# Hybrid decoder step: ten ring slots, convolution tables between weight parts, query rows behind loads, another order in the last attention step, Strassen blocks loaded in the projection

## Chip, cores and metric

The kernel runs on one core of one Trainium2 chip. The metric is the device time of one launch in microseconds (us).

## The reference

One layer (D_MODEL 1024, float32) for a prompt of 512 tokens and for 64 sample tokens (8 sequences of 8 tokens with a past of 4096 keys in pages). Cut to what matters:

```python
x = x + 0.5 * swiglu_ffn(rms_norm(x, g_ffn1), w_ffn1_in, w_ffn1_out)      # D_FF 2816
h = rms_norm(x, g_mix)
u, q, k, v, qi, ki, wi, gc, ga = project_in(h, w_in, g_q, g_k, pos)
conv = silu(layer_norm(depthwise31(u, state), g_cln, b_cln)) @ w_cout
idx  = top_k(index_scores(qi, wi, keys), k=min(256, n_keys // 4))        # a search by threshold
att  = gathered_attention(q, K[idx], V[idx]) @ w_aout                    # 8 heads x 64
x = x + (gc * conv + ga * att) @ w_o
x = x + 0.5 * swiglu_ffn(rms_norm(x, g_ffn2), w_ffn2_in, w_ffn2_out)
```

The new keys, values, indexer keys and the last rows of the convolution's input are outputs too.

## The kernel before

Every engine has one instruction stream written out by hand (the blocks `sp`, `pe`, `act`, `dve`, `pool`); nothing is scheduled by a planner. Semaphores order the engines, and what stands ahead of a waiting instruction on its engine decides when it runs. In order of time:

**A, 0 to 160 us, sample tokens.** The 64 sample tokens go through the first feed-forward part and `w_in`. The weights are read once, as 82 loads of 512 KB (`w_in`'s first four are smaller), which SyncE issues in `stream` (L369) into a ring of 6 slots; each waits until TensorE has used the load six places ahead of it (`ring_used`). TensorE multiplies them in `stream_mm` (L577). Between them it also transposes the prompt (`xnp`), sums its squares (L565) and transposes the cached indexer keys (`turn_ik`, L713). `x_sample` and the prompt's four blocks of 512 KB are issued at the start, by ScalarE.

**B, 160 to 208 us.** The sample tokens' index scores on TensorE.

**C, 205 to 652 us, prompt feed-forward 1**, as 68 units of 1024 weight columns by 128 rows, in three thirds. Each float32 weight is split in two parts of fewer bits, so a unit is a chain: SyncE's `load` (L377) brings `w_raw`, ScalarE (`hi`, L1234) makes `w_hi`, GpSimd (`lo`, L2547) or, in the last third, VectorE (`split_lo`, L1722) makes `w_lo`, and TensorE (L589) does three sets of products. `w_raw` has two slots, `w_lo` two. VectorE meanwhile runs the top-k search, and then, from unit 47 on, the keys of the sample attention: per token a product `kprod` (L2257) of gathered keys `kv` (GpSimd, L2613) with query rows `qb` (SyncE, L442), and a sum. The list `KEYS` gives the unit at which each token's turn comes, and `queries` in SyncE's stream sends the next row when the unit is far enough; four `qb` buffers, so a row waits on `kv_used`. UA = 68 is the first number after these units.

**D, 652 to 1106 us.** The projection of the prompt by `w_in` (`wn`, L969, L1003, L1116), attention of the prompt in 32 steps (logits, softmax on ScalarE as `Pp`, its transposes `pTp` from L1140, values L1150), and the convolution's taps on VectorE.

**E, 1106 to 1228 us.** Eight merge units (L544) for `w_aout` and `w_cout`, the convolution's layer norm (sums over channels by TensorE, L1159; `conv_mean_off` on VectorE, L2443 and L2445), and eight units of `w_o`. `t_hi` and `t_lo` are the parts of the attention's output `attT`.

**F, 1228 to 1634 us.** Feed-forward 2 with Strassen's seven products (L638) for ten blocks; GpSimd makes sums of weight blocks in `left_sums` (L2657 to L2667), VectorE splits them (L1749, L1754).

## Time and profile before

| | |
|---|---|
| median of 3 runs (lowest, highest) | 1648.18 us (1648.09, 1651.65) |
| the profiled execution | 1649.05 us, span of its records 1647.1 us |
| mean granted TensorE clock | 0.962 |
| PE busy / DVE / POOL / ACT | 1505.0 (91%) / 1105.2 (67%) / 574.4 (35%) / 497.9 us (30%) |
| DMA | 248.77 MB, 151 GB/s over the span |

PE is TensorE (matmuls), PEld its weight loads, DVE VectorE, ACT ScalarE, POOL GpSimd, SPq SyncE's DMA queue. A row `[9.06 <-POOL w_lo L2547]` says that the engine was idle 9.06 us before this instruction, and that w_lo, made by line 2547 on POOL, ended that. The difference of 1.95 us between the profiled execution's time and its span lies outside the records.

### The profile page before, as it was taken

The numbers are of one execution on the slowest core, as the hardware profiler recorded it, in microseconds if no ns is written. First come the engines' busy times: TensorE is split into PE (matmuls) and PEld (weight loads), VectorE is DVE, ScalarE is ACT, GpSimd is POOL, SyncE is SP. The second block draws the span as 40 slices with busy tenths as digits, with TensorE's granted clock in tenths as the row PEclk, the third lists the DMA queues.
The fourth block names the chain that finished last, engine by engine and source line by source line (L and its number), as shares of the span: only waits on it lengthen the run. The fifth ranks groups of instructions, "written<-read, shape, count | busy, mean of one in ns | idle before, by whom it ended". The sixth has DMA issues, their size and how long they took to land.

```text
span 1647.1 us, 20847 instructions
## 1 busy us (share of the span) xinstructions
PE 1505.0 (91%) x8219; PEld 1161.4 (71%) x8219; DVE 1105.2 (67%) x1688; ACT 497.9 (30%) x748; POOL 574.4 (35%) x412
## 2 busy tenths in 40 slices
PE   5877979889999987999999889978998899999998
PEld 2332358767888865544766555658998899999997
DVE  1615269999994688899868689843769755565222
ACT  3411422112211213122121444453346444454110
POOL 2000244335435855646216477112122355430000
PEclk9988989999999998999999899989999999999999
DMA  9897143222224787878528677232231222322222
GB/s 314 314 346 247 39 52 102 90 67 87 91 77 138 252 255 240 290 246 300 184 77 271 215 236 210 84 122 72 90 116 63 82 88 89 102 78 70 75 94 77
DMA packets 156275, 248.77 MB, mean 151 GB/s; under 512 B 11885, under 2 KB 104253, under 8 KB 155915
## 3 DMA queue, kind: packets, MB, share of 16 engines
q1 hardware_dynamic: 131006, 163.96, 31.0%
q0 software_dynamic: 23104, 76.16, 14.7%
q10 hardware_dynamic: 2069, 7.34, 1.2%
q8 instruction: 64, 1.05, 0.3%
q14 instruction: 32, 0.26, 0.0%
HBM read 237.58 MB, written 10.20 MB: 150 GB/s over the span
## 4 chain that ended last, share of the span: by engine, by line
PE 65%; DVE 17%; DMA 8%; issue 3%; ACT 3%; POOL 2%; ACTq 0%; SPq 0%; DVEq 0%; POOLq 0%
PE ps L638 13%; PE ps L589 11%; PE ps L654 8%; PE ps L1003 6%; PE ps L544 6%; PE ps L969 5%; DVE EQ L2103 4%; PE ps L1116 3%; DVE yacc L2419 2%; PE ps L783 2%; PE ps L577 2%; DVE kprod L2257 2%; DMA ring<-w_ffn_in 2%; PE ps L1020 1%; DMA w_raw<-w_ffn_out 1%
## 5 line engine op out<-in xcount | busy, mean ns | idle before, releaser
L2547 POOL TENSOR_TENSOR w_lo<-w_raw,w_hi 128x1024 fp32r<-128x1024 f32 x65 | 165.9, 2554 | 302.0 <-ACT w_hi L1234 301.8
L638 PE MATMUL ps<-bh,wqr 128*128 128x288 f32 x944 | 207.7, 297 | 4.5 <-DVE bl L1754 4.5
L1234 ACT ACTIVATE w_hi<-w_raw 128x1024 fp32r<-128x1024 f32 x88 | 91.4, 1040 | 351.5 <-PE ps L589 240.3
L2613 POOL DMA_INDIRECT kv<-cache_k,idxT x128 | 137.8, 1076 | 94.9 <-DVE kprod L2257 62.7
L2613 POOL DMA_INDIRECT kv<-cache_v,idxT x128 | 129.1, 1009 | 102.0 <-PE ps L1020 66.3
L638 PEld LDWEIGHTS ps<-bh,wqr 128*128 128x128 f32 x944 | 158.4, 190 | 4.7 <-issue 4.7
L589 PE MATMUL ps<-h_hi,w_hi 128*128 128x512 f32 x352 | 140.5, 399 | 12.7 <-POOL w_lo L2547 10.0
L589 PE MATMUL ps<-h_hi,w_lo 128*128 128x512 f32 x352 | 138.5, 394 | 0.0
L589 PE MATMUL ps<-h_lo,w_hi 128*128 128x512 f32 x352 | 138.4, 393 | 0.0
L654 PE MATMUL ps<-a_hi,wqr 128*128 128x288 f32 x704 | 121.6, 295 | 0.0
L1003 PE MATMUL ps<-h,wn 128*128 128x288 f32 x448 | 112.6, 412 | 3.1 <-DVE U_p L2089 1.9
L638 PE MATMUL ps<-bl,wqr 128*128 128x288 f32 x384 | 113.8, 296 | 0.0
L969 PE MATMUL ps<-wn,xg 128*128 128x512 f32 (+1 forms) x256 | 105.1, 570 | 3.6 <-DMA wn<-w_in 1.8
L1003 PEld LDWEIGHTS ps<-h,wn 128*128 128x128 f32 x448 | 85.5, 192 | 30.2 <-ACT sgb L1510 2.6
L654 PEld LDWEIGHTS ps<-a_hi,wqr 128*128 128x128 f32 x704 | 103.0, 188 | 0.0
L589 PE MATMUL ps<-a1h,w_hi 128*128 128x512 f32 x176 | 74.7, 424 | 22.9 <-DVE w_lo L1722 10.5
L969 PEld LDWEIGHTS ps<-wn,xg 128*128 128x128 f32 x256 | 49.7, 197 | 56.7 <-issue 49.6
L1762 DVE TENSOR_TENSOR wqr<-wq,wqr 128x1024 fp32r<-128x1024 f32 (+1 forms) x24 | 27.2, 1134 | 91.9 <-ACT wqr L1272 91.9
L589 PEld LDWEIGHTS ps<-h_hi,w_hi 128*128 128x128 f32 x352 | 67.1, 191 | 29.1 <-POOL w_lo L2547 10.6
L2657 POOL TENSOR_TENSOR wq<-wq 128x1024 f32<-128x1024 f32 x10 | 25.5, 2554 | 177.8 <-PE ps L638 135.2
L2257 DVE TENSOR_TENSOR kprod<-kv,qb 128x1024 f32<-128x1024 f32 x64 | 79.8, 1246 | 8.8 <-issue 2.7
L1116 PE MATMUL ps<-h,wn 128*128 128x288 f32 x320 | 84.4, 418 | 0.7 <-ACT sgb L1596 0.7
(477 smaller groups left out, 3288.8 us busy)
## 6 DMA issues: line engine op xcount, KB each, us to landing
w_raw<-w_ffn_in SPq DMA_DIRECT2D x48, 512.0 KB, 3.5
ring<-w_ffn_in SPq DMA_DIRECT2D x44, 512.0 KB, 7.0
wq<-w_ffn_in SPq DMA_DIRECT2D x40, 512.0 KB, 3.6
...
```

The costliest lines, as they stand in the source:

```text
L544: mm = pe.matmul(ps[:, 4 * half + 2 * m + hf_, 0:HALF], w[:, k, m * P:(m + 1) * P], x[:, kc0 + k, hf_ * HALF:(hf_ + 1) * HALF], start=(fir ...
L589: mm = pe.matmul(ps[:, 2 * half + m, :], w[:, k, m * P:(m + 1) * P], x[:, kc0 + k, c0:c0 + SEQ], start=(first and k == 0 and fst), stop=(l ...
L638: mm = pe.matmul(ps[:, bank + m, 0:HALF], w[:, k, m * P:(m + 1) * P], b[:, j, k, :], start=(j in (0, 1, 5) and k == 0 and fst), stop=(k == ...
L654: mm = pe.matmul(ps[:, 4 * half + 2 * m + hf_, 0:HALF], w[:, k, m * P:(m + 1) * P], x[:, kc0 + k, hf_ * HALF:(hf_ + 1) * HALF], start=(kc0 ...
L969: mm = pe.matmul(ps[:, s % 8, 0:n], xg[:, kk, P * b:P * b + P], wt[:, k, :], start=(kk == 0), stop=(kk == KD - 1))
L1003: mm = pe.matmul(ps[:, 4 * half + 2 * m + hf_, 0:HALF], wt[:, k, m * P:(m + 1) * P], h32[:, 4 * (n % 2) + k, hf_ * HALF:(hf_ + 1) * HALF], ...
L1116: mm = pe.matmul(ps[:, 2 * m + hf_, 0:HALF], wt[:, k, m * P:(m + 1) * P], h32[:, 4 * (n % 2) + k, hf_ * HALF:(hf_ + 1) * HALF], start=(n % ...
L1234: act.activation(w_hi[:, slot, 0:n], w_raw[:, slot, 0:n], ACT.Copy).then_inc(S_("hi_ready"), 1)
L2103: return dve.tensor_scalar(EQ[:, :], S[:, :], thr, 0.0, op, ALU.add, accum_out=dst)
L2257: dve.tensor_tensor(kprod[:, :, :], kv[:, n % KV, :, :], qb[:, j, :].unsqueeze(1).to_broadcast([P, 2, DA]), ALU.mult)\
L2547: pool.tensor_tensor(w_lo[:, slot, 0:n], w_raw[:, slot, 0:n], w_hi[:, slot, 0:n].bitcast(F32), ALU.subtract)\
L2613: pool.indirect_dma_start(kv[:, n % KV, c, :], None, rows[n // NS], bass.IndirectOffsetOnAxis(ap=idxT[:, c, t:t + 1], axis=0))\
```

## The change

**1. Stream of stage A.** The first 60 loads go around ten places instead of six: the ring's six, two in `w_raw`, and two in a new `spare` that lies over `w_lo`. The last 22 use the ring's six. `x_sample` is issued by SyncE ahead of the loads; the prompt's four blocks are issued by ScalarE after it has normed the sample tokens.

**2. Tables on GpSimd.** The four loads of the convolution's weights `wconv` (128 x 31 elements of 4 bytes), three small ones and a copy in HBM stand between the `lo` parts of units 4 to 9, not ahead of the one of unit 2.

**3. Query rows.** The row of `KEYS[n]` is sent from unit `KEYS[n]+4` on instead of `+3` (as long as that is below UA). VectorE's `prod(10)` comes ahead of the split of unit 61 (`w_lo`), not behind it.

**4. Last attention step.** On PE the convolution's sums come one step later; on ACT the last gate's high half and the `w_hi` of merge unit 1 come later, and that of merge unit 3 ahead of the four pairs of `silu` and `c_hi`; on DVE `t_lo` comes ahead of `conv_mean_off`.

**5. Strassen blocks.** The first four blocks (`wq`) are loaded behind six of the eight `w_o` loads, not behind all; their wait (`m_ready` 9) is the same.

**6.** `left_sums(2)` on GpSimd waits also for the seventh `bl` of block 1 (`h_ready`).

**7.** Some semaphores are merged with others (`qrep_ready`, `ends_taken`, `unat_done`, `state_kept`).

```diff
+        (spare,), _ = place(used["w_lo"][0], [("spare", (P, 2, 1024), F32)])
+        WIDE = 60
+        RING_AT = [i % 10 for i in range(WIDE)] + [i % RING for i in range(N_RING - WIDE)]
+        def ring_slot(i):
+            s = RING_AT[i]
+            return ring[:, s, :] if s < RING else (w_raw, spare)[(s - RING) // 2][:, (s - RING) % 2, :]
...
-                if i >= RING:
-                    sp.wait_ge(S_("ring_used"), i - RING + 1)
+                if RING_AT[i] in RING_AT[:i]:
+                    sp.wait_ge(S_("ring_used"), i - RING_AT[:i][::-1].index(RING_AT[i]))
...
-                while sent[0] < NS and (u >= ROWS_AT + 5 if sent[0] < 4 else KEYS[sent[0] - 4] + 3 <= u):
+                while sent[0] < NS and (u >= ROWS_AT + 5 if sent[0] < 4 else KEYS[sent[0] - 4] + (4 if KEYS[sent[0] - 4] + 4 < UA else 3) <= u):
...
+                if i == 2:
+                    sp.wait_ge(S_("m_ready"), KD + 1)
+                    for slot, kh, nh in ((A11, 0, 0), (A21[1], 0, 1), (A22[1], 1, 1), (A12[1], 1, 0)):
+                        sp.dma_start(wq[:, slot, :]...).then_inc(S_("w11_in"), 16)
...
-                if i == 33:
+                if i == 34:
                     pe.wait_ge(S_("mix_free"), 10)
                     conv_sums(0, yacc)
...
-            for b in range(4):
-                act.dma_start(xnp[:, b, :], inp["x_prompt"][P * b:P * (b + 1)]).then_inc(S_("xp_in"), 16)
...
             sample_norm(0)
+            for b in range(4):
+                act.dma_start(xnp[:, b, :], inp["x_prompt"][P * b:P * (b + 1)]).then_inc(S_("xp_in"), 16)
...
+                if i == 33:
+                    gate_high(7)
...
+            act.wait_ge(S_("ring_used"), N_RING + 39)
+            hi(UM + 1)
...
+                if v == out_unit(2, 0) - 1:
+                    prod(10)
...
-            conv_mean_off()
             for k in range(KA):
                 dve.wait_ge(S_("parts_hi"), k + 1)
                 dve.tensor_tensor(t_lo[:, k, :], attT[:, k, :], t_hi[:, k, :].bitcast(F32), ALU.subtract).then_inc(S_("t_ready"), 1)
+            conv_mean_off()
...
+                if 4 <= u < 4 + KC:
+                    pool.dma_start(wconv[:, u - 4, :], ...)
...
+                if i == 2:
+                    pool.wait_ge(S_("h_ready"), 2 * KD + 7)
```

GpSimd's stream at the start of stage C, before (`w_lo` is the part that `lo` makes, the first being that of unit 2; line numbers are each kernel's own):

```order
L2593 DMA causal<-c_causal 128x128
L2595 DMA wconv<-w_dw 128x31x1 x4
L2598 DMA bconv<-b_dw 128x4x1
L2598 DMA gcln<-g_cln 128x4x1
L2598 DMA bcln<-b_cln 128x4x1
L2599 DMA o_conv_sample<-state_conv 8x11264
L2547 TENSOR_TENSOR w_lo<-w_raw,w_hi 128x1024 [waits hi_ready] x46
```

And after:

```order
L2566 TENSOR_TENSOR w_lo<-w_raw,w_hi 128x1024 [waits hi_ready] x3
L2633 DMA wconv<-w_dw 128x31x1
L2566 TENSOR_TENSOR w_lo<-w_raw,w_hi 128x1024 [waits hi_ready]
L2633 DMA wconv<-w_dw 128x31x1
L2566 TENSOR_TENSOR w_lo<-w_raw,w_hi 128x1024 [waits hi_ready]
L2633 DMA wconv<-w_dw 128x31x1
L2566 TENSOR_TENSOR w_lo<-w_raw,w_hi 128x1024 [waits hi_ready]
L2633 DMA wconv<-w_dw 128x31x1
L2566 TENSOR_TENSOR w_lo<-w_raw,w_hi 128x1024 [waits hi_ready]
L2637 DMA bconv<-b_dw 128x4x1
L2637 DMA gcln<-g_cln 128x4x1
L2637 DMA bcln<-b_cln 128x4x1
```

Three parts now stand ahead of the first table, and one between each two of the next.

SyncE's stream in the last third of stage C, before (`w_ffn_out` with 4 x 256 and 2 x 256 columns are the two units of an output group, `qb` a query row):

```order
L442 DMA qb<-q_scratch 128x512 [waits kv_used]
L377 DMA w_raw<-w_ffn_out 128x4x256 [waits lo_ready]
L442 DMA qb<-q_scratch 128x512 [waits kv_used] x2
L377 DMA w_raw<-w_ffn_out 128x2x256 [waits lo_ready]
L442 DMA qb<-q_scratch 128x512 [waits kv_used] x2
L377 DMA w_raw<-w_ffn_out 128x4x256 [waits lo_ready]
L442 DMA qb<-q_scratch 128x512 [waits kv_used]
L377 DMA w_raw<-w_ffn_out 128x2x256 [waits lo_ready]
```

And after:

```order
L457 DMA qb<-q_scratch 128x512 [waits kv_used]
L394 DMA w_raw<-w_ffn_out 128x4x256 [waits lo_ready]
L457 DMA qb<-q_scratch 128x512 [waits kv_used]
L394 DMA w_raw<-w_ffn_out 128x2x256 [waits lo_ready]
L457 DMA qb<-q_scratch 128x512 [waits kv_used] x2
L394 DMA w_raw<-w_ffn_out 128x4x256 [waits lo_ready]
L457 DMA qb<-q_scratch 128x512 [waits kv_used] x2
L394 DMA w_raw<-w_ffn_out 128x2x256 [waits lo_ready]
```

Each row stands one load further back.

ScalarE's stream at the last attention step, before (`Pp` and `pTp` of the last two steps, `sgb` and `gate_scratch` the gate's high half, `attT` the attention's output):

```order
L1618 ACTIVATE pTp<-ps 128x512 [waits patt_done,pturn_done]
L1596 ACT_TABLE_LOAD
L1596 ACTIVATE sgb<-ps 128x576 [waits ring_used]
L1548 DMA gate_scratch<-sgb 128x1152 [waits mix_free,sgb_ready]
L1234 ACTIVATE w_hi<-w_raw 128x1024 [waits unit_used,raw1,ring_used]
L1611 ACTIVATE Pp<-Pp,small 128x512 [waits psum_ready]
L1618 ACTIVATE pTp<-ps 128x512 [waits patt_done,pturn_done]
L1624 ACTIVATE attT<-ps 128x128 [waits patt_done]
L1618 ACTIVATE pTp<-ps 128x512 [waits patt_done,pturn_done]
L1624 ACTIVATE attT<-ps 128x128 [waits patt_done]
L1654 ACTIVATE t_hi<-attT 128x576 [waits patt_evac,atts_evac]
L1654 ACTIVATE t_hi<-attT 128x576 x3
```

And after:

```order
L1635 ACTIVATE pTp<-ps 128x512 [waits patt_done,pturn_done]
L1628 ACTIVATE Pp<-Pp,small 128x512 [waits psum_ready]
L1635 ACTIVATE pTp<-ps 128x512 [waits patt_done,pturn_done]
L1641 ACTIVATE attT<-ps 128x128 [waits patt_done]
L1635 ACTIVATE pTp<-ps 128x512 [waits patt_done,pturn_done]
L1613 ACT_TABLE_LOAD
L1613 ACTIVATE sgb<-ps 128x576 [waits ring_used]
L1565 DMA gate_scratch<-sgb 128x1152 [waits mix_free,sgb_ready]
L1641 ACTIVATE attT<-ps 128x128 [waits patt_done]
L1669 ACTIVATE t_hi<-attT 128x576 [waits patt_evac,atts_evac]
L1669 ACTIVATE t_hi<-attT 128x576 x3
L1252 ACTIVATE w_hi<-w_raw 128x1024 [waits unit_used,raw1,ring_used]
```

The gate's table load, `sgb` and `w_hi` stood ahead of the last `Pp`; now the gate stands behind the last `pTp`, and `w_hi` behind `t_hi`.

## Rows read from the trace of the kernel before

**Rows 1.** The page, part 4: engines' shares of the chain that ended last.

```profile
PE 65%; DVE 17%; DMA 8%; issue 3%; ACT 3%; POOL 2%; ACTq 0%; SPq 0%; DVEq 0%; POOLq 0%
```

**Rows 2.** Windows of 5 us in the sample stream: span, busy time of each engine, clock, DMA.

```profile
35.00:40.00 5.00, 5.00 (x28) 2.06 (x28) 0.00 (x0) 4.71 (x10) 0.00 (x0) 1.00 0.62 202
...
50.00:55.00 5.00, 5.00 (x24) 1.80 (x24) 2.82 (x2) 0.63 (x1) 0.00 (x0) 1.00 0.22 61
60.00:65.00 5.00, 4.10 (x20) 1.14 (x20) 5.00 (x9) 2.52 (x4) 0.00 (x0) 1.00 1.05 395
...
75.00:80.00 5.00, 4.80 (x31) 2.48 (x31) 0.00 (x0) 2.45 (x5) 1.00 (x1) 1.00 0.51 135
...
100.00:105.00 5.00, 4.80 (x30) 2.29 (x30) 0.00 (x0) 2.21 (x5) 0.00 (x0) 1.00 0.53 167
```

**Rows 3.** Waits, 0 to 160 us: engine, line, releaser, total, times, longest.

```profile
PEld ps L577 <- DMA ring<-w_ffn_in: 28.4, 17, 3.7
```

**Rows 4.** Timelines of POOL, PE, DVE: start, busy, line, operation, count, [idle before, releaser].

```profile
214.31 5.23 POOL L2595 DMA_DIRECT2D wconv<-w_dw  x3
227.83 1.74 POOL L2595 DMA_DIRECT2D wconv<-w_dw  x1 [8.29 <-issue]
...
220.17 0.39 PE L589 MATMUL ps<-h_hi,w_hi 128*128 128x512 f32 x1
...
222.89 0.39 PE L589 MATMUL ps<-h_hi,w_hi 128*128 128x512 f32 x1
...
234.83 0.80 PE L589 MATMUL ps<-h_hi,w_hi 128*128 128x512 f32 x1 [9.06 <-POOL w_lo L2547]
...
247.51 0.69 DVE L2059 TENSOR_TENSOR prod<-silu,ps 128x512 f32<-128x512 f32 x1 [11.69 <-PE ps L589]
```

**Rows 5.** Waits, 565 to 652 us, then SyncE's queue, then the window.

```profile
ACT w_hi L1234 <- DMA w_raw<-w_ffn_out: 41.1, 7, 9.2
...
DVE w_lo L1722 <- ACT w_hi L1234: 18.2, 5, 5.3
...
SPq L442 <- DVE kprod L2257: 67.1, 17, 6.6
...
565.00:652.00 87.00, 70.98 (x272) 55.32 (x271) 68.31 (x71) 19.00 (x26) 50.94 (x48) 0.90 0.78 252
```

**Rows 6.** Timelines of ACT, DVE and PE at the last attention step.

```profile
1094.82 1.28 ACT L1596 ACT_TABLE_LOAD   x1
...
1097.30 1.06 ACT L1234 ACTIVATE w_hi<-w_raw 128x1024 fp32r<-128x1024 f32 x1 [0.53 <-ACT sgb L1596]
...
1106.22 2.77 DVE L2445 TENSOR_TENSOR yacc<-yacc,conv_mean 128x576 f32<-128x576 f32 x4
...
1101.17 4.15 PE L1159 MATMUL ps<-yacc,ones 128*128 128x288 f32 x16
...
1111.72 0.85 PE L544 MATMUL ps<-t_hi,w_hi 128*128 128x288 f32 x2 [5.39 <-DVE t_lo L2478]
...
1140.93 0.50 PE L544 MATMUL ps<-t_hi,w_hi 128*128 128x288 f32 x2 [3.39 <-POOL w_lo L2547]
```

**Rows 7.** Timelines of DVE and PE around the first Strassen block.

```profile
1202.74 1.54 DVE L1740 SCALAR_TENSOR_TENSOR h_lo<-xT,g2c,h_hi 128x576 fp32r<-128x576 f32 x2
...
1215.54 5.83 DVE L1740 SCALAR_TENSOR_TENSOR h_lo<-xT,g2c,h_hi 128x576 fp32r<-128x576 f32 x2
...
1228.32 0.82 PE L603 MATMUL ps<-h_hi,w_hi 128*128 128x288 f32 x2 [2.49 <-issue]
```

**Rows 8.** Timelines of POOL, DVE and PE in the seventh product.

```profile
1277.36 2.40 POOL L2667 TENSOR_TENSOR wq<-wq 128x1024 f32<-128x1024 f32 x1 [2.87 <-PE ps L638]
...
1268.77 3.50 DVE L1754 TENSOR_TENSOR bl<-blf,bh 128x1152 fp32r<-128x1152 f32 x1
...
1275.49 1.35 DVE L1754 TENSOR_TENSOR bl<-blf,bh 128x1152 fp32r<-128x1152 f32 x1
...
1284.63 0.58 PE L638 MATMUL ps<-bh,hrB 128*128 128x288 f32 x1 [4.20 <-DVE bl L1754]
```

More of the change, by code:

```diff
@@ L510, in _ @@
             vo = inp["w_o"].rearrange("o (k p) n -> p (o k) n", p=P)
-            with sp.Fori(0, 4) as i:
+            v1 = inp["w_ffn2_in"].rearrange("o (k p) n -> p (o k) n", p=P)
+            for i in range(4):
                 for j in range(2):
-                    load(UO + 2 * i + j, vo[:, 4 * j:4 * j + 4, bass.ds(i * 256, 256)], j, 1024)
+                    load(UO + 2 * i + j, vo[:, 4 * j:4 * j + 4, i * 256:i * 256 + 256], j, 1024)
+                if i == 2:
+                    sp.wait_ge(S_("m_ready"), KD + 1)
+                    for slot, kh, nh in ((A11, 0, 0), (A21[1], 0, 1), (A22[1], 1, 1), (A12[1], 1, 0)):
+                        sp.dma_start(wq[:, slot, :].rearrange("p (k n) -> p k n", k=4), v1[:, 4 * kh:4 * kh + 4, 256 + nh * FF:512 + nh * FF])\
+                            .then_inc(S_("w11_in"), 16)
             ffn(U2, inp["w_ffn2_in"], inp["w_ffn2_out"])
@@ L2275, in _ @@
                     out_add(1, 3)
-                if in_unit(8) <= v < out_unit(2, 0) and v % 4 == 3:
+                if in_unit(8) <= v < in_unit(10) and v % 4 == 3:
                     prod((v - in_unit(8)) // 4 + 8)
@@ L2593, in _ @@
             pool.dma_start(causal[:, :], con["causal"]).then_inc(S_("gain_in"), 16)
-            for k in range(KC):
-                pool.dma_start(wconv[:, k, :], inp["w_dw"][0, :, k * P:(k + 1) * P].rearrange("w p -> p w"), allow_slow_non_contiguous=True)\
-                    .then_inc(S_("gain_in"), 16)
-            for dst, name in ((bconv, "b_dw"), (gcln, "g_cln"), (bcln, "b_cln")):
-                pool.dma_start(dst[:, :], inp[name].rearrange("o (k p) -> p (o k)", p=P), allow_slow_non_contiguous=True).then_inc(S_("gain_in"), 16)
-            pool.dma_start(out["conv_sample"][:, :, 0:CW - 1 - NEW, :], inp["state_conv"][:, :, NEW:CW - 1, :]).then_inc(S_("state_kept"), 16)
             rows = [inp[name].rearrange("o n p h d -> (o n p) (h d)") for name in ("cache_k", "cache_v")]
@@ L2618, in _ @@
                 lo(u)
+                if 4 <= u < 4 + KC:
+                    pool.dma_start(wconv[:, u - 4, :], inp["w_dw"][0, :, (u - 4) * P:(u - 3) * P].rearrange("w p -> p w"), allow_slow_non_contiguous=True)\
+                        .then_inc(S_("gain_in"), 16)
+                if u == 4 + KC:
+                    for dst, name in ((bconv, "b_dw"), (gcln, "g_cln"), (bcln, "b_cln")):
+                        pool.dma_start(dst[:, :], inp[name].rearrange("o (k p) -> p (o k)", p=P), allow_slow_non_contiguous=True).then_inc(S_("gain_in"), 16)
+                if u == 5 + KC:
+                    pool.dma_start(out["conv_sample"][:, :, 0:CW - 1 - NEW, :], inp["state_conv"][:, :, NEW:CW - 1, :]).then_inc(S_("nat_out"), 16)
                 if u == ROWS_AT + 2:
```

57 lines of the change are left out of this document (26 added, 31 removed).

## The prediction

> **What bounds the kernel now.** I read first the shares of the chain that ended last [rows 1]: TensorE 65%, VectorE 17%, DMA 8%. So most of the time is matmuls that this change leaves as they are, and what can move is in the stretches where TensorE waits. I then went through the stages in order, with windows, waits and timelines, and looked at each wait of TensorE next to an edited place. There are four kinds.
>
> In stage A the weight stream is the bound, but it is interrupted. At 60 us, where TensorE only multiplies loads, the DMA engines move 395 GB/s and TensorE is busy 4.10 us of 5. In four other windows, where TensorE transposes or sums, TensorE is full and the DMA rate falls to 202, 61, 135 and 167 GB/s [rows 2]: the six slots are full of loads that are not used yet. Later TensorE waits for DMA: 28.4 us in 17 waits of its weight loads alone [rows 3]. In the first units of stage C, TensorE is idle for 9.06 us, since GpSimd issues the `wconv` tables ahead of the `w_lo` part [rows 4]. In the last third of stage C the chain is SyncE, ScalarE, VectorE, TensorE: SyncE's queue waits 67.1 us for `kprod` with query rows, ScalarE waits 41.1 us for `w_raw`, VectorE 18.2 us for `w_hi` [rows 5]. At the end of stage D TensorE waits 5.39 us for `t_lo`, and later 3.39 for GpSimd's part of merge unit 3 [rows 6].
>
> **Part 1, the stream.** What an idle link costs is the bytes not moved: against 395 GB/s the four windows lack 193, 334, 260 and 228, together 1015 GB/s for 5 us, so 5 x 1015 / 395 = 12.8 us [rows 2]. A load is 524,288 bytes, 1.33 us at 395 GB/s. Four more slots let the stream run 5.3 us longer into each interruption, and the idle parts of the four windows are 2.4, 4.2, 3.3 and 2.9 us, so each is covered. TensorE then finds ten loads, and does one in 0.82 us (20 matmuls, four to a load, in 4.10 us [rows 2]) where they arrive every 1.33, so it catches up and the link stays the bound. The prompt's blocks (2.1 MB, 5.3 us of the link) come behind the first ten loads: they are the same bytes, and what uses them is TensorE's interruptions, which are cover. I take -13. The small work of VectorE and ScalarE on the sample tokens behind the stream's end is the same as before and moves along. Lower gain: if only the deepest window is mended, and the others only moved, -4. Upper: the interruptions overlap wholly, and partly idle windows beside these are mended too, -18.
>
> By a rule of the Trainium skill ("DMA: Bandwidth & Descriptors", Specifications) one core's share of HBM is about 358 GB/s, and a stream near that has little to gain. The trace differs: 395 GB/s [rows 2]. By 358 the same four windows would lack 165, 297, 223 and 191, so 12.2 us in place of 12.8, and part 1 would end there.
>
> **Part 2, the tables.** TensorE starts unit 2 at 234.83 after 9.06 idle [rows 4]. GpSimd issued three tables in 5.23 us, stood 8.29 us, issued the fourth in 1.74, then the small ones. Without them `w_lo` of unit 2 follows its `w_hi` at once, unit 2 starts as unit 1 ends, and VectorE's first `prod` (idle 11.69 before 247.51) comes when the search has ended, 11.69 us before. So the gain lies between 9.06 and 11.69; unit 2 also came slower behind the pause (0.80 us for its first matmul against 0.39). I take -10.5; -12 and -2.5 (with the 8 us below) are the bounds. Each table is now 1.74 us of GpSimd between two parts. A part is 2.40 us [rows 8] (the same operation and size as a sum), and a unit 5.4 us (12 matmuls between the starts at 220.17 and 222.89 [rows 4], and it has 24), so 4.1 of 5.4 is used. GpSimd could issue the fourth table 13.5 us after it began the first, which I read as the time that three need in the queue: 4.5 us each, under 5.4, so I expect that they don't pile up. A weight load beside a table takes longer, however. What it costs if the cover is gone: up to 2 us per table, 8 us.
>
> **Part 3, query rows.** Each `w_raw` load stood behind a row that waits for a buffer; it now stands behind the row of one unit before. The stretch of 87 us has TensorE busy 70.98 and VectorE 68.31, so it could be 16 us shorter at the most, and VectorE's 18.2 us in 5 waits are nearly all that it is idle [rows 5]. The longest, 5.3, is the first, before the third's first split, where VectorE isn't yet late for TensorE; the other four hold 12.9. `w_hi` then still waits for a load that takes its time to land, and VectorE's keys and splits come in uneven pieces, so I leave a quarter of these waits: -9.5. Rows sent later could make `kprod` wait; with four buffers each is sent some three tokens ahead, so I cost it at nothing, and at 2 us if it isn't hidden. The end of the third starts the next stage, which is bounded by TensorE, so the gain stays. Lower gain -4 (rows and loads land together), upper -16, by TensorE's busy time.
>
> **Part 4, last attention step.** Ahead of the last `Pp` on ScalarE stood the gate's high half and a `w_hi`, from the table load at 1094.82 to the end of `w_hi` at 1098.36, 3.5 us; on TensorE the sums of 4.15 us stood ahead of the last values; on VectorE `conv_mean_off` (2.77) ahead of `t_lo` [rows 6]. TensorE's first merge unit starts at 1111.72. The new chain: the last `Pp` and `pTp` come some 2.5 of the 3.5 us earlier (VectorE's quotient holds the rest), 4.15 goes, and of `conv_mean_off` some 1.6 count, since `t_hi` wasn't ready before. Against it the gate's 2.5 us (3.5 less the `w_hi` of 1.06) now stand ahead of `attT`; TensorE's last values cover most, I count 1.0. So -2.5 - 4.15 - 1.6 + 1.0 = -7.2. The sums of 4.15 move into the wait. The 3.39 us at 1140.93 go because `w_hi` of unit 3 no longer stands behind the `silu` loop: -3.4. Matmuls behind a long pause are slower (two in 0.85 us behind 5.39 idle, two in 0.50 behind 3.39 [rows 6]), so shorter pauses save about 1. Together -11.5, between -7 (TensorE waits for GpSimd's `w_lo` of unit 1, whose `w_hi` is later) and -13.
>
> **Part 5, Strassen blocks.** Now VectorE's `h_lo` takes 5.83 us where the same work took 1.54, while GpSimd makes its sums; TensorE pauses 2.49 [rows 7]. The blocks come some 13 us earlier, so the sums collide with the split and squares of the unit before: late by about 2.6 there, for 2.49 removed and its lower clock. -0.5, between -3.5 (no collision left) and +2.5.
>
> What the Trainium skill says ("SBUF — State Buffer", the section on two separate sides) is that a VectorE instruction with two SBUF inputs and a GpSimd one share a port pair, which one holds for a whole instruction. The trace agrees, 5.83 against 1.54 [rows 7]. By that rule a moved sum only moves the collision, and this part would be worth 0.
>
> **Part 6, `left_sums(2)`.** `bl` took 3.50 us beside a sum and 1.35 without; three of VectorE's instructions are stretched so, 2.15 each, ahead of product 7, which waits 4.20 [rows 8]. With the sums held back that product starts up to 6.4 us earlier, but the next block's first product then waits for three sums of 2.40, 7.2 us, beside which product 7 and a split run. -1.5, between -3.5 (half of the sums hidden behind product 7) and +1 (7.2 spent for 6.4). Part 7 waits for things that are done: 0.
>
> **Sum.** -13 - 10.5 - 9.5 - 11.5 - 0.5 - 1.5 = -46.5, on the profiled execution's 1649.05 (span 1647.1 and 1.95 around it): 1602.5. The runs' median is 0.9 below that, so 1602 when rounded for it.
>
> **The rivals.** (a) *The stream gains little*: the ten slots fill, but the prompt's blocks and the small tables share the link, and ScalarE's and VectorE's sample work sets the end. For it: TensorE's stops come again after each interruption. Against: 28.4 us waited for DMA [rows 3]. Part 1 is then -4, and the time 1611. (b) *The last third stays bound by loads*: ScalarE waited 41.1 us for `w_raw` [rows 5], more than VectorE for it, and the query rows use the link too. Part 3 gives -2 and part 4 -9: 1612. (c) *More than the sum*: VectorE's earlier keys let the projection and the convolution's taps start early, so part 3 gives its bound of -16, and the clock stays up for 1.5 more. The time would be 1594. (d) *Slower*: the tables don't fit between parts. GpSimd's 8.29 us pause [rows 4] is then taken in front of `w_lo` at each table, and the weight loads beside them queue behind 4-byte elements. Against the gain of 46.5 it takes more than 6 such events of 8.3 us (50 us); four tables, three small ones and a copy are 8. At 8 it gives 1602 + 66 = 1668; it decides from 6 on. Against it: three of the four tables went out in 5.23 us.
>
> **Chances.** The forecast 0.60, (a) 0.14, (b) 0.12, (c) 0.06, (d) 0.04, and 0.04 for (d) with 5 or 6 of its pauses, which ends within 0.3% (4.9 us, about what a measurement of this kernel can tell). So faster 0.92, same 0.04, slower 0.04. The sum's bounds are -18 - 12 - 16 - 13 - 3.5 - 3.5 = -66 and -4 - 2.5 - 4 - 7 + 2.5 + 1 = -14; not all ends come together, so the range goes from 1590 to 1623, which takes in (a) to (c).
>
> **What would show it.** Right: in the windows of the stream the DMA rate stays near 390 GB/s and stage B starts at about 147; TensorE has no pause of 9 us after unit 1 and VectorE's first `prod` comes as the search ends; SyncE's queue still waits for `kprod`, but ScalarE's wait for `w_raw` shrinks below 25 us; the first merge unit follows the last attention step by under 3 us idle. Wrong: a pause of TensorE before units 5 to 10 with `w_raw` or `w_lo` as releaser; index scores that start later than 152; `kprod` waiting for `qb`; a new wait for `hi(UM+1)` in the merge units.

## The result, and the profile after

| | before | changed |
|---|---|---|
| median (lowest, highest), 4 runs each | 1649.91 us (1648.09, 1653.53) | 1604.92 us (1597.52, 1606.32) |
| profiled execution's span | 1647.1 us | 1604.3 us |

The ratio is 0.9724 (95% interval 0.9693 to 0.9755), so the kernel became 45 us faster. The forecast was 1602. The page's first lines for the changed kernel are its span, and busy time of each engine:

```profile
span 1604.3 us, 20812 instructions
...
PE 1494.0 (93%) x8219; PEld 1156.8 (72%) x8219; DVE 1100.0 (69%) x1688; ACT 499.0 (31%) x748; POOL 570.7 (36%) x412
```

TensorE has nearly the same work (1494.0 us against 1505.0, at a mean granted clock of 0.968 against 0.962), so most of the gain is idle time that went. To see where, I took single matmuls that exist in both kernels, the k-th of its kind, and compared when each starts. How much earlier it starts is the lead. The matmuls must keep their place in TensorE's order: at the convolution's sums, which part 4 moves one step back, the lead would read 30.91, though the transposes just ahead have 29.94. The lead of the changed kernel, in the two profiled executions:

| matmul, by its time before | lead, us | part | gain of the part | forecast |
|---|---|---|---|---|
| 133.25, sample's new x | 6.91 | 1 | 6.9 | 13 |
| 216.96, unit 0 of stage C | 7.84 | | 0.9 | |
| 361.06, output units of the first third | 21.24 | 2 | 13.4 | 10.5 |
| 519.99 | 21.06 | | -0.2 | |
| 663.63, behind stage C | 31.85 | 3 | 10.8 | 9.5 |
| 1094.94, transposes of `Pp`, last group but one | 29.94 | | -1.9 | |
| 1148.09, merge units | 42.37 | 4 | 12.4 | 11.5 |
| 1232.07, feed-forward 2 begins | 42.12 | 5 | -0.3 | 0.5 |
| 1300.06, second block | 43.07 | 6 | 1.0 | 1.5 |
| 1635.20, last transposes | 43.07 | | 0 | |

**Part 1.** The 5-us windows of the changed kernel, against [rows 2]:

```profile
35.00:40.00 5.00, 4.70 (x28) 2.60 (x30) 0.00 (x0) 4.45 (x10) 0.00 (x0) 1.00 1.05 388
50.00:55.00 5.00, 5.00 (x22) 1.76 (x22) 2.49 (x2) 0.63 (x1) 0.00 (x0) 1.00 0.58 190
60.00:65.00 5.00, 5.00 (x26) 1.60 (x24) 5.00 (x9) 2.46 (x5) 0.00 (x0) 1.00 1.04 391
75.00:80.00 5.00, 5.00 (x26) 3.52 (x26) 0.00 (x0) 3.36 (x7) 0.26 (x1) 0.64 0.49 154
80.00:85.00 5.00, 5.00 (x26) 1.72 (x24) 1.37 (x2) 0.62 (x1) 0.75 (x1) 1.00 0.71 268
100.00:105.00 5.00, 5.00 (x24) 1.57 (x22) 0.00 (x0) 0.28 (x1) 0.00 (x0) 1.00 1.05 385
```

At 35 us the link now runs at 388 GB/s (202 before), at 100 at 385 (167). But at 50 it falls to 190, and at 75 and 80 to 154 and 268: ten slots are full there too. At 75 us it is no longer the number of slots that counts. TensorE's timeline:

```profile
73.35 5.49 PE L734 MATMUL ps<-ident,ikn 128*128 128x128 f32 x24 [5.84 <-ACT ikT L1388]
...
126.34 1.09 PE L780 MATMUL ps<-ident,xs 64*128 64x64 f32 x8 [3.18 <-DVE xs L1969]
```

TensorE has done its loads and waits 5.84 us for ScalarE, which has to evacuate the first transposed indexer keys (`turn_ik`). ScalarE's timeline, and then VectorE's, show why:

```profile
68.58 0.63 ACT L1376 ACTIVATE a_s<-a_s 64x512 f32<-64x512 f32 x1 [0.63 <-DVE a_s L1919]
...
72.19 0.63 ACT L1376 ACTIVATE a_s<-a_s 64x512 f32<-64x512 f32 x1 [2.71 <-DVE a_s L1919]
72.72 1.05 ACT L1388 ACTIVATE ikT<-ps 128x512 f32<-128x512 f32 x2
```

```profile
53.20 3.35 DVE L1940 RECIPROCAL rstd<-rstd 128x512 f32<-128x512 f32 x1 [0.70 <-ACT rstd L1394]
...
65.63 1.47 DVE L1944 TENSOR_TENSOR h_lo<-hfp,h_hi 128x512 fp32r<-128x512 f32 x2
67.13 0.69 DVE L1918 COPY tmps<-ps 64x512 f32<-64x512 f32 x1
```

ScalarE copies `ikT` at 72.72, behind the silu of sample columns 3 at 72.19; that stands in its stream behind columns 2 at 68.58, and this waits for VectorE's fold, which begins at 67.13, when the norm of the prompt (from 53.20, last `h_lo` at 65.63) is done. The norm starts when the prompt's sums end, 51.67 us, no earlier than before (51.34).

**Part 2.** GpSimd's timeline, then TensorE's and VectorE's at unit 2:

```profile
219.82 2.40 POOL L2566 TENSOR_TENSOR w_lo<-w_raw,w_hi 128x1024 fp32r<-128x1024 f32 x1 [3.95 <-ACT w_hi L1252]
...
226.69 1.78 POOL L2633 DMA_DIRECT2D wconv<-w_dw  x1
229.81 2.39 POOL L2566 TENSOR_TENSOR w_lo<-w_raw,w_hi 128x1024 fp32r<-128x1024 f32 x1 [1.33 <-ACT w_hi L1252]
232.15 2.01 POOL L2633 DMA_DIRECT2D wconv<-w_dw  x1
...
246.13 1.74 POOL L2633 DMA_DIRECT2D wconv<-w_dw  x1 [2.14 <-issue]
```

```profile
217.51 0.39 PE L610 MATMUL ps<-h_hi,w_hi 128*128 128x512 f32 x1
```

```profile
228.69 1.29 DVE L2076 TENSOR_TENSOR prod<-silu,ps 128x512 f32<-128x512 f32 x2
```

A table is 1.74 to 2.01 us of GpSimd between parts of 2.4, and TensorE's first matmul of unit 2 comes at 217.51 without a pause; `prod` follows the search without idle time. The fourth table still stood 2.14 us before it went out, and it stands 2.0 to 2.2 us in the ten other kernels that space the tables. The next `w_lo` part starts right behind it, at 247.89, and TensorE has no wait between 216 and 270 us: what is buffered covers it. That removed the 9.06 and, at VectorE, the 11.69 us of [rows 4]. The rest of the 13.4 is in the search behind it. VectorE's groups (count; busy, mean ns) before, for 248 to 322 us, and then of the changed kernel for the same work:

```profile
L2068 DVE TENSOR_TENSOR a1l<-prod,a1h 128x512 fp32r<-128x512 f32 x8 | 9.5, 1230 | 0.1
...
L2065 DVE CAST a1h<-prod 128x512 fp32r<-128x512 f32 x8 | 5.0, 667 | 0.6
```

```profile
L2082 DVE CAST a1h<-prod 128x512 fp32r<-128x512 f32 x8 | 6.4, 847 | 0.6
L2085 DVE TENSOR_TENSOR a1l<-prod,a1h 128x512 fp32r<-128x512 f32 x8 | 5.2, 688 | 0.1
```

The same eight `a1l` take 5.2 us in place of 9.5 and the `a1h` 6.4 in place of 5.0, 2.9 us less together, since other instructions now meet GpSimd's `w_lo` parts: VectorE does the same 136 instructions in 71.1 us instead of 74.0.

**Part 3.** The same waits as [rows 5], over the 73 us that the stretch of 87 has become, then SyncE's, then the window:

```profile
ACT w_hi L1252 <- DMA w_raw<-w_ffn_out: 6.9, 3, 5.8
...
DVE w_lo L1739 <- ACT w_hi L1252: 5.9, 3, 3.1
```

```profile
SPq L457 <- DVE kprod L2274: 32.0, 18, 4.2
```

```profile
544.00:617.00 73.00, 65.76 (x274) 51.72 (x272) 66.66 (x69) 18.89 (x26) 51.92 (x46) 0.98 0.88 287
```

SyncE's wait for `kprod` fell from 67.1 to 32.0 and ScalarE's for `w_raw` from 41.1 to 6.9; VectorE waits 5.9 us for `w_hi`, not 18.2, and is busy 66.66 us of 73. The step is 10.8 us here and in the repetition below, where TensorE's granted clock is at its lower level (0.50) for 3.4 us shortly ahead of the matmul at 663.63. In seven other kernels with this part that stretch comes behind it and the step is 12.5; at 680 us both groups have 11.4.

**Part 4.** TensorE, against [rows 6]: the sums, the first merge unit, and unit 3.

```profile
1070.26 4.15 PE L1177 MATMUL ps<-yacc,ones 128*128 128x288 f32 x16 [0.87 <-ACT sgb L1613]
1074.57 0.53 PE L565 MATMUL ps<-t_hi,w_hi 128*128 128x288 f32 x2 [0.16 <-DVE t_lo L2496]
...
1100.08 0.52 PE L565 MATMUL ps<-t_hi,w_hi 128*128 128x288 f32 x2 [1.20 <-DVE gate_a L2509]
```

0.16 us idle ahead of the first merge unit, 5.39 before; 1.20 ahead of unit 3, not 3.39, and now VectorE's `gate_a` ends it. In leads: 7.2 us come up to the first merge unit (29.94 to 37.15), 2.7 of them already at the last transposes, and 2.2 at unit 3. The other 3.0 are clock: the granted clock of the kernel before is 0.50 (1.2 GHz) from 1108.3 to 1115.1 and from 1142.4 to 1145.8 us, beginning in a pause of TensorE and 1.5 us behind one, and the changed kernel has 1.00 (2.4 GHz) throughout the same work.

**Part 5.** VectorE, then TensorE, against [rows 7]:

```profile
1159.24 3.33 DVE L1739 TENSOR_TENSOR w_lo<-w_raw,w_hi 128x1024 fp32r<-128x1024 f32 x1
1162.50 5.81 DVE L1757 SCALAR_TENSOR_TENSOR h_lo<-xT,g2c,h_hi 128x576 fp32r<-128x576 f32 x2
```

```profile
1173.15 0.53 PE L565 MATMUL ps<-m_hi,w_hi 128*128 128x288 f32 x2 [2.49 <-DVE w_lo L1739]
```

`h_lo` is stretched as before (5.81, 5.83), and the `w_lo` ahead of it as well, 3.33 us. The pause of 2.49 us has moved from the start of feed-forward 2 to a unit of `w_o`. A stretch of lower clock has moved with it (the third number from the end is the granted clock):

```profile
1174.31:1177.70 3.39, 3.39 (x17) 3.39 (x16) 3.33 (x5) 2.59 (x4) 0.00 (x0) 0.50 0.67 208
```

Before, the clock was lower for 3.4 us from 1227.7 on, from within the old pause. By the rule of the Trainium skill that was cited ("SBUF — State Buffer", on two separate sides) VectorE or GpSimd holds their shared port pair for a whole instruction. The trace agrees, with these 5.81 and 3.33 us: the moved sums met other instructions of VectorE.

**Part 6.** VectorE, GpSimd and TensorE, against [rows 8]:

```profile
1235.53 1.35 DVE L1771 TENSOR_TENSOR bl<-blf,bh 128x1152 fp32r<-128x1152 f32 x1
...
1244.37 3.28 DVE L1766 TENSOR_TENSOR wqr<-wq,wqr 128x1024 fp32r<-128x1024 f32 x1 [6.82 <-POOL wq L2686]
```

```profile
1237.06 2.39 POOL L2680 TENSOR_TENSOR wq<-wq 128x1024 f32<-128x1024 f32 x1 [66.50 <-DVE bl L1771]
...
1241.92 2.35 POOL L2686 TENSOR_TENSOR wq<-wq 128x1024 f32<-128x1024 f32 x1
```

```profile
1247.70 0.61 PE L659 MATMUL ps<-bh,wqr 128*128 128x288 f32 x1 [6.57 <-DVE wqr L1766]
```

All `bl` are short now (1.35 us). But GpSimd's sums start when the last of them is made, three take 7.2 us, VectorE waits 6.82 us for the third and TensorE 6.57 for VectorE.

### The profile page after: what moved, and what is told of

It is laid out like the page before. It is cut to its first block and busy times, and to the rows that moved or that the text cites. A ratio compares the mean times of both kernels' runs of the same rounds, so it can differ in the third digit from the quotient of the medians.

```text
span 1604.3 us, 20812 instructions
## 1 busy us (share of the span) xinstructions
PE 1494.0 (93%) x8219; PEld 1156.8 (72%) x8219; DVE 1100.0 (69%) x1688; ACT 499.0 (31%) x748; POOL 570.7 (36%) x412
## 5 line engine op out<-in xcount | busy, mean ns | idle before, releaser
L2626 POOL DMA_INDIRECT kv<-cache_k,idxT x128 | 141.7, 1107 | 81.2 <-DVE kprod L2274 48.4
L989 PEld LDWEIGHTS ps<-wn,xg 128*128 128x128 f32 x256 | 50.2, 199 | 58.1 <-issue 47.8
L2438 DVE SCALAR_TENSOR_TENSOR yacc<-U_p,wconv,yacc 128x512 f32<-128x512 f32 x120 | 82.2, 747 | 2.0 <-DVE bias_new L2358 0.5
## 6 DMA issues: line engine op xcount, KB each, us to landing
ring<-w_ffn_out SPq DMA_DIRECT2D x14, 512.0 KB, 11.4
```

Source lines behind the costliest of these rows:

```text
L989: mm = pe.matmul(ps[:, s % 8, 0:n], xg[:, kk, P * b:P * b + P], wt[:, k, :], start=(kk == 0), stop=(kk == KD - 1))
L2438: link(dve.scalar_tensor_tensor(out=yacc[:, k, NS:NT], in0=U_p[:, k, j:j + SEQ], scalar=wj, in1=yacc[:, k, NS:NT], op0=ALU.mult, op1=ALU.add))
L2626: pool.indirect_dma_start(kv[:, n % KV, c, :], None, rows[n // NS], bass.IndirectOffsetOnAxis(ap=idxT[:, c, t:t + 1], axis=0))\
```

## The experiments

All are the changed kernel with one edit, unless said otherwise. The lead at the matmuls of the table above, in us, each from its profiled execution:

| kernel | 133 | 217 | 361 | 520 | 664 | 1095 | 1148 | 1232 | 1300 |
|---|---|---|---|---|---|---|---|---|---|
| changed | 6.9 | 7.8 | 21.2 | 21.1 | 31.9 | 29.9 | 42.4 | 42.1 | 43.1 |
| u1_ring6 | -2.0 | -1.1 | 12.9 | 12.8 | 22.4 | 21.2 | 33.6 | 34.9 | 36.4 |
| u2_prompt_early | 8.2 | 9.0 | 22.9 | 22.9 | 35.3 | 34.5 | 46.9 | 49.2 | 50.2 |
| u3_tables_first | 8.1 | 10.9 | 11.0 | 10.9 | 23.4 | 25.0 | 37.4 | 37.5 | 38.5 |
| n1_ik_first | 12.6 | 15.9 | 29.9 | 29.7 | 42.2 | 41.1 | 53.6 | 53.6 | 54.3 |
| u4_rows_early | 7.9 | 8.9 | 22.2 | 22.1 | 22.3 | 20.3 | 32.7 | 32.5 | 33.6 |
| u5_last_step_old | 7.3 | 10.4 | 24.3 | 24.4 | 36.9 | 38.7 | 34.5 | 36.5 | 37.7 |
| u6_blocks_late | 8.4 | 11.9 | 25.6 | 25.6 | 38.1 | 39.0 | 51.4 | 53.8 | 55.4 |
| u7_sums_free | 8.2 | 11.2 | 25.1 | 25.0 | 37.5 | 35.8 | 48.2 | 50.5 | 52.7 |

Read each row for differences from column to column: what one edit does stands between two columns, and the rest of a row shows how much two executions of the same code differ. u1 to u3 and n1 ran together on one chip, u4 to u7 together on a second; the changed kernel's 1604.92 is from neither run, so times are best compared among the kernels of one group.

**Six slots again.**

```diff
-        RING_AT = [i % 10 for i in range(WIDE)] + [i % RING for i in range(N_RING - WIDE)]
+        RING_AT = [i % RING for i in range(N_RING)]
```

> The changed kernel with the stream back on six slots; everything else as changed (x_sample first, the prompt's blocks behind the sample norm). In the changed kernel the transposes of the sample's new x start at 126.34 us, before at 133.25. Theory: the four more slots give this 6.9 us. Then these transposes go back to 132 to 134 us and the whole takes 6 to 8 us more than the changed kernel's 1604.9. Rival: the gain comes from the order of x_sample and the prompt's blocks, since the sample's first matmul starts 2.6 us earlier. Then the transposes stay below 129 us and the time below 1608.

1612.3 us, ratio 0.977 (0.9731 to 0.9808). The sample's x comes at 135.21 us, 8.9 later than in the changed kernel and 2.0 later than before. Nine executions with the changed stage A have leads of 6.2 to 8.4 here, so the slots give 8.2 to 10.4 us, more than the theory's 6.9. What is left of the change at six slots is 2.0 us slower than before; that the later loads of the prompt are the reason is likely, but no run has them later by themselves on six slots. The rival falls.

**The prompt's blocks at the start.**

```diff
             act.dma_start(ident[:, :], con["ident"]).then_inc(S_("const_in"), 16)
+            for b in range(4):
+                act.dma_start(xnp[:, b, :], inp["x_prompt"][P * b:P * (b + 1)]).then_inc(S_("xp_in"), 16)
...
             sample_norm(0)
-            for b in range(4):
-                act.dma_start(xnp[:, b, :], ...)
```

> The changed kernel, but the prompt's four blocks are issued at the start again, ahead of the sample norm. Theory: the first 30 us are bounded by the link, which must bring the same bytes before the prompt's transposes either way, so the transposes of the prompt (31.53 us) move by less than 1.5 us, those of the sample's x (126.34) by less than 1.5, and the time stays within 2 us. Rival: the blocks behind the ring's loads come too late and hold the prompt's sums and all that VectorE does behind them; then the sums (44.54 us) come 3 or more us earlier and the time falls by 3.

1600.03 us, ratio 0.9706 (0.9669 to 0.9744). The prompt's sums start at 43.31 (44.54 in the changed kernel), and the lead at 133 is 8.2, among the 6.2 to 8.4 of the executions that share the changed stage A. No effect that can be told from two executions of one code; the theory holds for the starts. The median is 4.9 us under the changed kernel's, not within 2, but no kernel with the prompt's blocks late and all else unchanged ran beside it.

**Tables ahead of unit 2 again** (the three small ones and the copy too).

```diff
             pool.dma_start(causal[:, :], con["causal"]).then_inc(S_("gain_in"), 16)
+            for k in range(KC):
+                pool.dma_start(wconv[:, k, :], ...)
...
```

> The changed kernel with the wconv tables, the small ones and the copy back ahead of the w_lo of unit 2. Theory: TensorE's pause of some 9 us before unit 2 comes back, VectorE's first prod waits some 11.5 us, and its a1l instructions in the search stage are longer again by 2.9 us in sum, since they meet GpSimd's parts; together 13 to 14.5 us more. Rival: the forecast's own size, 10.5, with no difference in the collisions.

1617.97 us, ratio 0.982 (0.9781 to 0.986). TensorE's pause is back:

```profile
223.86 0.79 PE L610 MATMUL ps<-h_hi,w_hi 128*128 128x512 f32 x1 [9.25 <-POOL w_lo L2566]
```

From 217 to 361 this kernel gains 0.1 us on the kernel before, the changed one 13.4. The eight `a1l` take 9.5 us again. So part 2 is 13.3 us, with the collisions, and the theory holds.

**Indexer keys ahead of the silus on ScalarE.**

```diff
             evac_a(0)
-            silu_s(2)
             evac_a(1)
-            silu_s(3)
             evac_ik(0)
+            silu_s(2)
+            silu_s(3)
```

> The changed kernel, and on ScalarE the evacuation of the first eight groups of transposed indexer keys stands ahead of the silu of sample columns 2 and 3 (these wait for VectorE, which norms the prompt until 67 us). Theory: the stream gained 6.9 and not 13 because TensorE now waits 5.84 us at the second pair of those transposes for ScalarE, behind VectorE's norm of the prompt, while the ten slots are full. Then this wait goes, the transposes of the sample's x start 3 to 5 us earlier than 126.34, and the time falls by 3 to 5 us. Rival: the link is the bound and makes up for the pause by its ten slots; then the start moves by less than 1 us.

1595.39 us, ratio 0.9672 (0.9636 to 0.9709). TensorE, and the windows at 75 and 80 us:

```profile
69.97 1.15 PE L734 MATMUL ps<-ident,ikn 128*128 128x128 f32 x8 [0.20 <-ACT ikT L1388]
74.54 0.69 PE L721 MATMUL ps<-ident,a_s 64*128 64x64 f32 x4 [3.42 <-DVE a_s L1932]
...
120.63 0.71 PE L780 MATMUL ps<-ident,xs 64*128 64x64 f32 x8 [3.19 <-DVE xs L1969]
```

```profile
75.00:80.00 5.00, 5.00 (x21) 1.59 (x21) 2.95 (x5) 0.90 (x2) 0.00 (x0) 0.72 1.11 430
80.00:85.00 5.00, 5.00 (x34) 2.03 (x32) 2.70 (x4) 1.01 (x2) 0.00 (x0) 1.00 0.98 342
```

The transposes run through; what remains is 3.42 us for the sample's `a_s`, and the link moves 430 and 342 GB/s (154 and 268). The sample's x comes at 120.63, 5.7 earlier than in the changed kernel and 4.5 earlier than in u2 and u3, which were run with it. This is the direct test of what held part 1 at half its forecast: the edit moves no load and adds no slot.

**Query rows early, prod(10) late.**

```diff
-                ... KEYS[sent[0] - 4] + (4 if KEYS[sent[0] - 4] + 4 < UA else 3) <= u):
+                ... KEYS[sent[0] - 4] + 3 <= u):
...
-                if v == out_unit(2, 0) - 1:
-                    prod(10)
```

(and `prod(10)` in its old place)

> The changed kernel with the query rows one unit earlier again (ahead of the weight load of their unit) and VectorE's prod(10) behind the split of unit 61. Theory: the load behind a waiting row was what made ScalarE and then VectorE late; the shift of TensorE against the kernel before stays at its value of 520 us through the last third, and the whole takes 10 to 12 us more than the changed kernel (from -21.1 to -34.9 at the third's end, -31.9 behind the next stage's start). Rival: VectorE's earlier start of the third (from parts 1 and 2) gives a part of it; then less than 6 us come back.

1613.62 us, ratio 0.9797 (0.9774 to 0.982). The lead stays at 22.1 us at 520 and 22.3 at 664, where those of u5 to u7 beside it grow by 12.5, and it takes 14.2 us more than u7. So 12 us are this part's, as the theory says, and the rival falls. ScalarE's wait, over 544 to 630 us, is as before the change:

```profile
ACT w_hi L1252 <- DMA w_raw<-w_ffn_out: 40.0, 8, 9.2
```

**The last attention step in its old order** (`conv_sums` at 33, `gate_high` and `hi(UM+1)` at 31, `merge_hi(UM+3)` behind the loop, `conv_mean_off` ahead of `t_lo`).

```diff
-                if i == 34:
+                if i == 33:
                     pe.wait_ge(S_("mix_free"), 10)
                     conv_sums(0, yacc)
```

> The changed kernel with the last attention step in the old order on all three engines, and the w_hi of merge unit 3 behind the silu loop. Theory: 11.4 us come back: some 7 in the wait for t_lo ahead of the first merge unit (0.16 us now, 5.39 before) with the convolution's sums of 4.15 us in front, some 3.5 in a wait before merge unit 3, the rest as lower clock behind them. Rival: the order isn't what counts, since VectorE or the gate's transfer ends last there; then TensorE waits as long and less than 5 us come back.

1611.62 us, ratio 0.9784 (0.9756 to 0.9812). TensorE at the sums, the first merge unit and unit 3, and a window:

```profile
1063.79 5.54 PE L1177 MATMUL ps<-yacc,ones 128*128 128x288 f32 x16
...
1075.73 0.85 PE L565 MATMUL ps<-t_hi,w_hi 128*128 128x288 f32 x2 [5.38 <-DVE t_lo L2497]
...
1105.46 0.82 PE L565 MATMUL ps<-t_hi,w_hi 128*128 128x288 f32 x2 [3.39 <-POOL w_lo L2566]
```

```profile
1059.82:1066.64 6.82, 5.76 (x18) 4.42 (x19) 0.00 (x0) 1.68 (x4) 2.31 (x1) 0.50 0.75 254
```

Both waits of [rows 6] are back to 0.01 us. The lead goes from 38.7 to 34.5 between 1095 and 1148, where the changed kernel's grows by 12.4; so 16.6 us came back there, 4.2 more than it had gained on the kernel before and 5.2 more than the theory. The 4.2 are clock. The granted clock of this execution is 0.50 for 20.5 us of the stretch (1059.8 to 1066.6, 1073.5 to 1080.3, 1104.2 to 1111.0), that of the kernel before for 10.2. In the first of these windows the sums run, 5.54 us for what took 4.15 at 1.00 [rows 6], and 2.7 of the 4.2 are lost there. Each of the three begins in a pause of TensorE. So part 4 is worth 12.4 us against one execution of the old order and 16.6 against another.

**Strassen blocks behind all eight loads.**

```diff
-                if i == 2:
+                if i == 3:
                     sp.wait_ge(S_("m_ready"), KD + 1)
```

> The changed kernel with the four Strassen blocks loaded behind all eight w_o loads. Theory: GpSimd's sums only meet other VectorE work: the wait of 2.49 us for w_lo at 1173 us goes, one of the same size comes before the first block of feed-forward 2, and the time stays within 1.5 us of the changed kernel. Rival: there is a gain of 2 to 4 us in the earlier load, since the stretched h_lo no longer stands in front of feed-forward 2; then this kernel is that much slower.

1596.0 us, ratio 0.9699 (0.9674 to 0.9725). Neither was right. The pause at a unit of `w_o` goes, and the one at the start of feed-forward 2 is shorter than the 2.49 us before the change:

```profile
1175.79 0.50 PE L624 MATMUL ps<-h_hi,w_hi 128*128 128x288 f32 x2 [1.33 <-issue]
```

The lead grows by 2.4 us between 1148 and 1232. With the blocks early it changes by -0.3 to 0.2 us in four kernels' executions (changed, u3, u4, n1) and by 1.3 to 2.3 in seven (u1, u2, u5, u7 and three of those below). What parts the two groups is mainly the clock: in the four it is 0.50 for 3.4 us right behind the pause at the unit of `w_o`, in the seven it stays at 1.00, behind pauses of the same size (2.1 to 2.5 us in both groups). So loading early costs 0.1 to 1.2 us where the clock stays up, and 2.3 to 2.7 where it doesn't.

**Sums not held back.**

```diff
-                if i == 2:
-                    pool.wait_ge(S_("h_ready"), 2 * KD + 7)
```

> The changed kernel without the wait for the seventh low part in left_sums(2). Theory: the changed kernel gained 1.0 us here (from 42.1 to 43.1 less than before between 1250 and 1300 us), since its product 7 ends 10 us sooner but the next block's product then waits 6.57 us for the split of GpSimd's sum. So this kernel is 0.5 to 2 us slower, with waits of 4 to 5 us at the sixth and seventh product again and none of 6.57. Rival: the wait only moves the stall and costs 1 us or more; then this kernel is faster by that.

1599.41 us, ratio 0.9718 (0.9695 to 0.974). TensorE in the sixth and seventh product:

```profile
1221.88 0.58 PE L659 MATMUL ps<-bh,wqr 128*128 128x288 f32 x1 [4.47 <-DVE bl L1771]
...
1232.41 0.37 PE L659 MATMUL ps<-bh,hrB 128*128 128x288 f32 x1 [1.94 <-issue]
```

The wait of 4.47 us at the sixth is back, the one of 4.20 at the seventh is 1.94, and none of 6.57. From 1232 to 1300 the lead grows by 2.2 us; with the wait it grows by 0.8 to 1.6 in the changed kernel and the ten others that have it. So the rival's direction holds, at the lower end of its size: the added wait costs 0.7 to 1.5 us, read from leads, since in the medians it is within the noise. What part 6 seemed to gain on the kernel before isn't its own: without its wait the step is 2.2 us.

**The last four** ran on a chip on which every kernel takes longer (before 1674.34 us), mostly between 740 and 1100 us: there TensorE has pauses of about 2 us without a releaser in the trace, and its mean clock is 0.79 from 740 to 780 us (1.00 in the changed kernel's first profile). Only differences among them are used. First the changed kernel again:

> The changed kernel as it is, for comparison on this chip. In its profiled execution stage B took 51.1 us and TensorE lost 4.6 us between 908 and 1068 us against the kernel before; five variants with the same code there lost at most 3.2 us and mostly under 2. Theory: these are differences between executions, so here the profile ends 1595 to 1602 us and the ratio lies at 0.969 to 0.972. Rival: they belong to the kernel, and the profile ends at 1604 again.

1623.05 us against 1674.34, ratio 0.971 (0.9662 to 0.9757). The theory's ratio holds. Its absolute time can't be judged on this chip, but stage B and the start of C gave a lead of 9.6 us at 217 and 23.1 at 361, against the kernel before on the other chip, so the 7.8 and 21.2 of the first profile were perhaps on the low side.

**Three changes together** (n1, u6 and u7):

> The changed kernel with three things put together: indexer keys evacuated ahead of silu 2 and 3 on ScalarE, Strassen blocks behind all eight w_o loads, no wait for the seventh low part in left_sums(2). Theory: the three lie in different stages and add up, 4.5 + 2.6 + 1 = 8 us less than the changed kernel in this job, ratio to before 0.964 to 0.967. Rival: what is won in the stream is lost in the gathers or the search behind it; then less than 4 us.

1616.87 us, ratio 0.9676 (0.963 to 0.9723). 6.2 us under the changed kernel in medians and 5.5 in the spans of the profiles (1612.5, 1618.0): of the 8 expected, 4.2 are there at 217 us, 0.4 in part 5 and 0.7 in part 6; 2.3 more come between 217 and 664, and between 664 and 1095 it loses 3.0 to the changed kernel. The ratio lies just outside the expected 0.964 to 0.967. The intervals of the two ratios overlap, so that it beats the changed kernel is likely, not shown.

**All tables in a row behind unit 4** (the three small ones and the copy too).

```diff
-                if 4 <= u < 4 + KC:
-                    pool.dma_start(wconv[:, u - 4, :], ...)
+                if u == 4:
+                    for k in range(KC):
+                        pool.dma_start(wconv[:, k, :], ...)
...
```

> The changed kernel with all four wconv tables, the three small ones and the copy between the w_lo parts of units 4 and 5. Theory: it is the spacing that hides the tables: in a row GpSimd stands 8 us for the fourth, as before the change, and TensorE waits 6 to 10 us at unit 5 or 6; VectorE's search runs on meanwhile, so its next prod waits. The whole takes 5 to 10 us more than the changed kernel. Rival: it was the place alone (not ahead of unit 2, where nothing is buffered); then 2 us at the most.

1637.32 us, ratio 0.978 (0.9728 to 0.9831), 14.3 more than the changed kernel beside it. GpSimd, and TensorE at unit 5:

```profile
227.21 5.50 POOL L2634 DMA_DIRECT2D wconv<-w_dw  x3
240.99 1.73 POOL L2634 DMA_DIRECT2D wconv<-w_dw  x1 [8.28 <-issue]
```

```profile
247.95 0.80 PE L610 MATMUL ps<-h_hi,w_hi 128*128 128x512 f32 x1 [13.44 <-POOL w_lo L2566]
```

Three tables go out in 5.5 us and the fourth after 8.28, as in [rows 4], and TensorE waits 13.44 us: more than the 9.06 of the kernel before, and more than the 6 to 10 expected, as the 14.3 in all is more than 5 to 10. VectorE's next `prod` waits as well, 14.31 us. The rival falls: it is the spacing that hides the tables, not the place alone. This is the mechanism of the forecast's rival (d), made to happen once.

**Query rows early alone** (`prod(10)` stays):

> The changed kernel with the query rows one unit earlier again, prod(10) staying where the change put it. With both undone 11 us came back. Theory: the rows ahead of the loads are nearly all of it, so 9 us or more come back here. Rival: prod(10) ahead of the first split matters as well; then 3 to 7 us come back.

1635.43 us, ratio 0.9772 (0.972 to 0.9824), 12.4 more than the changed kernel. Between 520 and 664 us the lead falls by 0.9 us, where the repetition's grows by 10.8. So the theory holds: the rows are all of part 3 that can be told, and `prod(10)` has no share above the noise.

## Why the prediction was right

The time, 1604.9, lies 2.9 us from the forecast 1602. The sizes of the parts agree less well than that: part 1 gave 6.1 us less than forecast, parts 2 to 4 together 5.1 more. That these nearly cancel is luck. The rest is parts 5 and 6 (1.3 short) and the steps that belong to no part (-1.2 in sum). The mechanisms of parts 2, 3 and 4 were right; the cover that part 1 counted on wasn't there.

- *Part 1, forecast 13, measured 6.9.* The step that failed is "so each is covered": the idle parts of the four windows were set against 5.3 us of lookahead, as if TensorE would go on once it had its ten loads. The windows at 35 and 100 us were mended; the one at 75 wasn't, since it was TensorE that waited, 5.84 us, for a chain on ScalarE and VectorE that starts with the prompt's sums and didn't move. n1 takes the chain apart and gets 4.5 more. Rival (a) named "ScalarE's and VectorE's sample work" as what would set the end, with the gain at 4; what happened lies between it and the forecast. The ring's own share is 8.2 to 10.4 us (u1). In the estimate by the 358 GB/s of the Trainium skill ("DMA: Bandwidth & Descriptors", Specifications) one of the four windows lacks 156, not 165, and the result is 12.1 us. The changed kernel moves more than that in a window, 388 and 385 GB/s.
- *Part 2, forecast 10.5, measured 13.4.* The pause and its place were right. That tables of 4.5 us don't pile up at one per unit of 5.4 was nearly right: the fourth stood 2.14 us, which the buffered parts covered (t_burst shows what happens if they don't). So 4.5 us for each is not what holds the queue, and what does stays open. Left out: VectorE, with the search, is the bound up to the first output units, where TensorE waited 4.2 us for `a1l` before and 0.9 now. So fewer collisions with GpSimd count there, 2.9 us.
- *Part 3, forecast 9.5, measured 10.8*, 12.5 in seven other kernels. Right, by the mechanism named: u4 and q_rows_only each give all of it back. A quarter of the four later waits, which sum to 12.9, was to stay (9.7 by that, rounded down); less did.
- *Part 4, forecast 11.5, measured 12.4.* The 7.2 at the first merge unit came as forecast. Unit 3 gave 2.2 and not 3.4, since another wait of 1.20 took over, and the clock 3.0 and not 1. Set against u5 the part is 16.6, so how well the sum of its terms fits is partly luck of the one profile.
- *Part 5, forecast 0.5, measured -0.3*, and by u6 between -0.1 and -2.7 against not doing it. The forecast's words, late by 2.6 there for 2.49 removed, describe the pause (its step in the lead is 2.8). The term that was mis-sized is "its lower clock", counted as removed: it came along with the pause, 1.5 us. And with the blocks late the pause before feed-forward 2 is only 1.33 us and has no lower clock behind it; that wasn't seen, and why it is shorter stays open.
- *Part 6, forecast 1.5, measured 1.0*, the size by luck. The trade of 4.47 and 4.20 for 6.57 was foreseen, but u7 shows that the wait is a loss of about 1 us. The forecast's own terms said so too: up to 6.4 us won for 7.2 spent; the -1.5 rested on sums hidden behind product 7, which by the wait of 6.57 us they mostly weren't.
- The shown signs: ScalarE's wait for `w_raw` under 25 us (6.9), first merge unit under 3 us idle (0.16), no wait of `kprod` for `qb`, no pause before units 5 to 10, no wait for `hi(UM+1)`: as forecast. Two signs of part 1 failed: the DMA rate was to stay near 390 GB/s and fell to 190, 154 and 268 in three windows, and stage B was to start at about 147 us and did at 153.86, above the 152 that was to show the forecast wrong.
